# Next gate product ahead of the down products, the sample maps' factor in ScalarE's copy, and two convolution steps on GpSimd

## The chip, the cores and the metric

One NeuronCore of a Trainium2 chip runs the whole program. The metric is device microseconds of one execution. TensorE (PE in the profile), VectorE (DVE), ScalarE (ACT) and GpSimd (POOL) each run their own instruction stream in order, SyncE (SP) issues weight loads, and the streams meet through semaphores.

## The reference, cut to what matters

One layer of a decoder for 1024 prompt tokens and 8 x 4 sample tokens, width 1024. Four mixers (a gated convolution, pooling, sparse top-k attention, differential attention) are followed by an output projection, then this gated MLP of width 2816, then a gated embedding:

```python
xn2 = rmsnorm(h, W['norm_ffn'][i])
g_conv, new_ffn = causal_dwconv(ffn_buf, xn2 @ W['w_gate'][i], W['conv_ffn'][i])   # 3 taps along tokens
h = h + (jax.nn.silu(g_conv) * (xn2 @ W['w_up'][i])) @ W['w_down'][i]
# differential attention: two softmax maps, the second times -lambda
a = probs(q1, k1) - lam * probs(q2, k2);  o = a @ v;  y_d = rmsnorm(o, subln) * (1 - lam_init)
```

## The kernel before, in words

Tokens are split: part a is the first 384 (`NA`), part b the other 672. In the middle of the program two things run interleaved on all engines: the **mixers** of part b, and the **dense** work, which there is the MLP of part a. The MLP has 22 chunks `f` of 128 hidden columns. Of each, TensorE makes a gate product (`"g"`), an up product (`"u"`), and, per 4 chunks (f below `FSPLIT` = 12) or per 2 chunks (from 12 on), 8 down products (`"d"`) that are added to the residual `H`. Chunks below 12 multiply in plain fp32 (8 products of 384 columns, 16 records in the trace); later ones use a high/low split of weights and rows, 24 products, and each weight block must first be split by ScalarE (`wh`, L596) and VectorE (`wl`, L603).

`QUANTA` lists the products in the order in which TensorE makes them, and alternate products use two PSUM banks (`bank(6 + n % 2)`). So product n first waits until product n-2 is read out (`freed`): a gate product by ScalarE's copy (`ag_cp`, L927), an up product by VectorE's multiplication (`a_mul`, L993), a down product by VectorE's addition into `H` (`h_ffn_a`, L977). In between, for each chunk, VectorE convolves the gate row (`dve_gate_conv`: the last two columns are kept in `gtail` L1021, first tap L1022, two more taps L1023 and L1024), ScalarE takes a tanh (L932), VectorE multiplies (L985, then L993 with the up product).

The interleaving is written out by a planner. The mixers' items are numbered n; each has four **places** (p = 0 to 3), and every engine's stream is generated place by place, so an engine does all its work of one place before that of the next. `ISSUED` spreads the dense products over places by their columns; the tables `FREE_AT`, `CONV_AT`, `TANH_AT`, `MUL_AT` and so on give each step of a chunk its place: about one place after what it needs, or earlier when a limit (the place where product n+2 starts) comes first. In one place an engine does `*_free` first, then the mixers' part, then `*_dense`; in a ScalarE place before the change the top-k counting (`act_stage`, L1386) belongs to the mixers' part.

The mixers: in stage one (places 156 to 251) part b runs differential attention with 20 prompt items and 4 sample items (`sdiff`), beside the bitwise top-k search, whose 31 steps are shared by VectorE (L1317) and ScalarE (L1386). In stage two (from place 252) it runs the sparse attention, and the MLP chunks from 12 on. For each item PE makes logits (place 4n), VectorE masks and takes maxima, ScalarE exponentiates (4n+2), VectorE combines the maps (`dve_finish`, 4n+3, for `sdiff` L1866 scales 64 x 1056 values), PE transposes (4n+6, 4n+7), ScalarE copies them (L1726, L1728), PE multiplies by values (4n+9). For tiles of prompt items VectorE's `dve_tile` makes squares, GpSimd a power (L1983), VectorE the product (L1889).

GpSimd's stream (`pool_mixers`) also issues in place order the DMAs that fetch pages of keys and values (L2034, L2042, L2049, L2050) through registers.

## Time and profile before

| what | value |
|---|---|
| three runs | 1745.3, 1760.32, 1759.58 us, median 1759.58 |
| profiled execution | 1758.01 us, of which the trace spans 1756.3 us |
| PE busy | 1630.0 us (93%), mean granted clock 0.969 |
| DVE busy | 1121.2 us (64%) |
| ACT busy | 682.9 us (39%) |
| POOL busy | 214.2 us (12%) |
| chain that ended last | PE 72%, DVE 14%, issue 6%, ACT 6% |

Busy time is the union of an engine's instructions. In the trace stage one lies at about 436 to 752 us from the start of the span and stage two at 752 to 1042 us; what follows is the output projection, the MLP and the embedding of part b. A line number with an engine names an instruction by the source line that issued it; many PE products share L859, and are told apart by their operands.

### The profile page before, as it was taken

To read this page: it belongs to the slowest core of one execution; us is meant where nothing else is said; L and a number is where in the kernel's file an instruction comes from. 1 tells how busy PE (TensorE), PEld (TensorE's weight loads), DVE (VectorE), ACT (ScalarE), POOL (GpSimd) and SP (SyncE) were. 2 spreads that over 40 slices of the span, in tenths; PEclk is the share of its full clock that TensorE was granted. 3 is DMA by queue.
4 is the path that set the end of the run, shared out by engine and by line. 5 is a ranking of instruction groups with operands and counts; after the bars stand their busy time and mean duration, and the time that the engine had idled before them with its cause. 6 is when DMAs were issued, how large, how long until landed. Compare 5 with 4: busy or idle time off the path is not lost.

```text
span 1756.3 us, 26856 instructions
## 1 busy us (share of the span) xinstructions
PE 1630.0 (93%) x9433; PEld 1393.2 (79%) x9433; DVE 1121.2 (64%) x2415; ACT 682.9 (39%) x1289; POOL 214.2 (12%) x360
## 2 busy tenths in 40 slices
PE   6989998998979898899889989899999999999996
PEld 5978897973535445467687889899999999999995
DVE  6466866377788978875556564655555555556845
ACT  5333443354367367433333433432222222223531
POOL 1000000031313222353331010000000000000000
PEclk9999999998989998999989999999999999999998
DMA  5331222241524323323222133122221222222313
GB/s 195 120 108 49 61 79 74 70 156 61 178 76 129 115 93 103 108 63 96 79 91 71 60 114 113 63 73 88 70 69 69 70 71 72 72 72 86 99 61 111
DMA packets 52815, 158.32 MB, mean 90 GB/s; under 512 B 9776, under 2 KB 13872, under 8 KB 52704
## 3 DMA queue, kind: packets, MB, share of 16 engines
q1 hardware_dynamic: 37840, 121.37, 20.6%
q0 software_dynamic: 14864, 35.53, 6.6%
q8 instruction: 62, 1.02, 0.2%
q14 instruction: 49, 0.40, 0.1%
HBM read 147.10 MB, written 9.76 MB: 89 GB/s over the span
## 4 chain that ended last, share of the span: by engine, by line
PE 72%; DVE 14%; issue 6%; ACT 6%; DMA 1%; POOL 0%; SPq 0%; DVEq 0%; POOLq 0%; ACTq 0%
PE ps L859 26%; PE ps L2116 22%; PE ps L2303 9%; DVE junk_b L1317 3%; PE ps L1582 2%; PE ps L1536 2%; ACT act_junk L1386 2%; PE ps L1613 1%; DVE Pb_b L1826 1%; PE ps L1191 1%; DVE wl L603 1%; PE ps L2477 1%; ACT wh L596 1%; DVE SC L1223 1%; PE ps L1593 1%
## 5 line engine op out<-in xcount | busy, mean ns | idle before, releaser
L603 DVE TENSOR_TENSOR wl<-wr,wh 128x1024 fp32r<-128x1024 f32 x176 | 215.3, 1223 | 247.9 <-ACT wh L596 247.3
L596 ACT ACTIVATE wh<-wr 128x1024 fp32r<-128x1024 f32 x176 | 186.1, 1057 | 443.7 <-PE ps L2116 222.3
L2116 PE MATMUL ps<-xh_b,wh 128*128 128x336 f32 x960 | 305.9, 319 | 7.4 <-DVE wl L603 3.3
L2116 PE MATMUL ps<-xl_b,wh 128*128 128x336 f32 x960 | 306.2, 319 | 0.0
L2116 PE MATMUL ps<-xh_b,wl 128*128 128x336 f32 x960 | 304.4, 317 | 0.0
L2116 PEld LDWEIGHTS ps<-xh_b,wh 128*128 128x128 f32 x960 | 182.0, 190 | 9.1 <-DVE wl L603 4.0
L2116 PEld LDWEIGHTS ps<-xh_b,wl 128*128 128x128 f32 x960 | 182.1, 190 | 0.0
L2116 PEld LDWEIGHTS ps<-xl_b,wh 128*128 128x128 f32 x960 | 181.8, 189 | 0.0
L859 PE MATMUL ps<-x_a,wr 128*128 128x384 f32 x384 | 150.8, 525 | 4.2 <-DVE H L977 4.2
L859 PE MATMUL ps<-xh_a,wh 128*128 128x384 f32 x400 | 139.5, 349 | 9.6 <-ACT H L900 3.9
L859 PE MATMUL ps<-xl_a,wh 128*128 128x384 f32 x400 | 137.5, 344 | 0.8 <-DVE H L977 0.8
L859 PE MATMUL ps<-xl_b,wh 128*128 128x336 f32 x352 | 114.8, 326 | 0.0
L859 PE MATMUL ps<-xh_b,wh 128*128 128x336 f32 x352 | 114.5, 325 | 0.0
L859 PE MATMUL ps<-xh_b,wl 128*128 128x336 f32 x352 | 114.1, 324 | 0.0
L859 PEld LDWEIGHTS ps<-x_a,wr 128*128 128x128 f32 x384 | 70.3, 200 | 52.7 <-issue 22.3
L1317 DVE TENSOR_SCALAR_CACHE_REDUCE junk_b<-SC,tk_b 32x1056 uint16<-32x1056 uint16 (+7 forms) x105 | 107.5, 1024 | 6.7 <-DMA SC<-score_spill 3.0
L2303 PE MATMUL ps<-al_b,wh 128*128 128x336 f32 x352 | 111.6, 317 | 0.0
L2303 PE MATMUL ps<-ah_b,wh 128*128 128x336 f32 x352 | 111.3, 316 | 0.2 <-DVE H L2387 0.2
L2303 PE MATMUL ps<-ah_b,wl 128*128 128x336 f32 x352 | 111.4, 316 | 0.0
L1386 ACT ACTIVATE act_junk<-SC,tk_b 128x1024 bf16<-128x1024 uint16 (+2 forms) x93 | 93.4, 1004 | 40.2 <-DVE tk_b L1367 29.0
L2387 DVE TENSOR_TENSOR H<-H,ps 128x336 f32<-128x336 f32 x176 | 85.0, 501 | 33.3 <-PE ps L2303 31.4
L859 PEld LDWEIGHTS ps<-xh_a,wh 128*128 128x128 f32 x400 | 75.9, 190 | 21.9 <-issue 15.0
(420 smaller groups left out, 3153.7 us busy)
## 6 DMA issues: line engine op xcount, KB each, us to landing
wr<-in_weights SPq DMA_DIRECT2D x212, 512.0 KB, 3.4
pages<-in_d_pages POOLq DMA_DIRECT2D x64, 128.0 KB, 2.4
values<-in_d_pages POOLq DMA_DIRECT2D x64, 128.0 KB, 2.5
pages<-in_c_pages POOLq DMA_DIRECT2D x128, 32.0 KB, 2.1
H<-in_xT SPq DMA_DIRECT2D x8, 336.0 KB, 9.1
H<-in_xT POOLq DMA_DIRECT2D x8, 336.0 KB, 5.9
out_y<-Y_out_b SPq DMA_DIRECT2D x8, 336.0 KB, 2.3
H<-in_xT SPq DMA_DIRECT2D x8, 192.0 KB, 4.9
```

Source lines behind the costliest of these rows:

```text
L596: nc.scalar.activation(wh[:, slot], wr[:, slot], ACT.Copy).then_inc(w_hi, 1)
L603: nc.vector.tensor_tensor(wl[:, slot], wr[:, slot], wh[:, slot].bitcast(f32), ALU.subtract).then_inc(w_lo, 1)
L859: last = nc.tensor.matmul(out[:, cols], w, x, start=j == 0, stop=j == count - 1)
L1191: last = nc.tensor.matmul(bank(2 * (u % 2) + h)[:, 0:w], Z[r, QI + p, i * P:(i + 1) * P], Z[r, KI2, a:a + w], start=True, stop=True)
L1223: last = nc.vector.scalar_tensor_tensor(dst, r[:, h], weight, dst, ALU.mult, ALU.add)
L1317: return nc.vector.tensor_scalar(self.junk[0:rows, 0:S], src, scalar, 0.0, op, ALU.add, accum_out=self.col(CNT, j, rows))
L1386: nc.scalar.activation(out[:, 0:S], self.half(j, k >= 15), ACT.Sign, bias=self.col(NBIAS, j), accum_out=self.col(CNT, j)).then_inc(self.ac ...
L1536: last = nc.tensor.matmul(flat(u + m)[:, a:a + w], H[part, q, i * P:(i + 1) * P], Z[part, k, a:a + w], start=True, stop=True)
L1582: last = nc.tensor.matmul(bank(5)[:, HD * h:HD * h + HD], pt[:, b * P:(b + 1) * P], v, start=b == 0, stop=b == i)
L2116: last = nc.tensor.matmul(bank(first_bank + c)[:, 0:CB], w, x, start=k == 0 and t == 0, stop=k == KC - 1 and t == 2)
L2303: last = nc.tensor.matmul(down_bank(v), w, x, start=q == 0 and t == 0, stop=q == 1 and t == 2)
L2387: nc.vector.tensor_tensor(cols, cols, down_bank(v), ALU.add).then_inc(h_ffn, 1)
```

## The change

Four edits. (1) The order of the products: before it was g(f), u(f), downs; now the gate product of the next chunk follows u(f) and stands ahead of the down products, except over the border between chunks 11 and 12 and after chunk 21. The weight blocks follow the same order, and the planner's tables are derived from the new list. (2) For `sdiff` items VectorE no longer scales the 64 x 1056 map: it makes the factor only, at place 4(n+1)+1 and no longer 4n+3, and ScalarE's copy of the 64 x 256 output is given it as scale. The transposes of `sdiff` and `dsa` items wait for the exponentials and no longer for VectorE. (3) From chunk 1 on GpSimd makes the first tap and the copy of the last two columns; VectorE waits for the tap, ScalarE's tanh for the copy. (4) ScalarE's counting goes to the end of each place, behind the dense part; the last product of a differential tile (L1889) goes from place p = 2 to the end of p = 3.

```diff
-for f in range(FC):
-    ...
-    add_chunk(f)
-    if 4 <= f < FSPLIT:
+def add_downs(f):
+    if f == FSPLIT - 1 or 4 <= f < FSPLIT:
         add_down(f // 4 - 1, f % 4)
     elif f >= FSPLIT + 2:
         add_down(down_of(f) - 1, f % 2)
     elif f >= FSPLIT:
         add_down(QUADS - 1, 2 + f - FSPLIT)
+
+for f in range(FC):
+    ...
+    if f in (0, FSPLIT) or not (1 if f < FSPLIT else 1):
+        add_product("g", f)
+    add_product("u", f)
+    if (1 if f < FSPLIT else 1) and f + 1 not in (FSPLIT, FC):
+        add_product("g", f + 1)
+    add_downs(f)
@@ act_dense
                 act.wait_ge(ag_conv, f + 1)
+                if f:
+                    act.wait_ge(ag_tail, f)
                 nc.scalar.activation(ge_a[:, f % 2, 2:2 + NA], gv_a[:, f % 2, 0:NA], ACT.Tanh).then_inc(ag_tanh, 1)
+        def pool_gate_tap(pool, f):
+            e, v, w = ge_a[:, f % 2], gv_a[:, f % 2, 0:NA], half_conv[:, 3 * f:3 * f + 3]
+            pool.wait_ge(ag_conv, f)
+            pool.wait_ge(ag_cp, f + 1)
+            if f >= 2:
+                pool.wait_ge(a_mul, f - 1)
+            nc.gpsimd.tensor_scalar(v, e[:, 0:NA], w[:, 0:1], None, ALU.mult).then_inc(ag_tap, 1)
+            nc.gpsimd.tensor_copy(gtail[:, f], e[:, NA:NA + 2]).then_inc(ag_tail, 1)
@@ dve_gate_conv
-            nc.vector.tensor_copy(gtail[:, f], e[:, NA:NA + 2])
-            link(nc.vector.tensor_scalar(v, e[:, 0:NA], w[:, 0:1], None, ALU.mult))
+            if f:
+                dve.wait_ge(ag_tap, f)
+            else:
+                nc.vector.tensor_copy(gtail[:, f], e[:, NA:NA + 2])
+                link(nc.vector.tensor_scalar(v, e[:, 0:NA], w[:, 0:1], None, ALU.mult))
@@ pe_transposes
-                pe.wait_ge(combined, real(n) + 1)
+                pe.wait_ge(exp_done if kind in ("sdiff", "dsa") else combined, real(n) + 1)
@@ act_sample
-                last = nc.scalar.activation(so_rows[0:64, :], use_at(("so", n))[0:64, 0:256], ACT.Copy)
+                act.wait_ge(combined, real(n) + 1)
+                factor = cf[0:64, 2 * (n % 2):2 * (n % 2) + 1]
+                last = nc.scalar.activation(so_rows[0:64, :], use_at(("so", n))[0:64, 0:256], ACT.Copy, scale=factor)
@@ dve_maxima
-                dve.wait_ge(combined, real(n))
+                dve.wait_ge(combined, real(n) - (ITEMS[n - 1][0] == "sdiff"))
@@ dve_finish
-                    link(nc.vector.tensor_tensor(k, k, small[0:rows, 33:34], ALU.mult))
-                nc.vector.tensor_scalar(logits(n)[0:rows, 0:NK], logits(n)[0:rows, 0:NK], k, None, ALU.mult).then_inc(combined, 1)
+                    nc.vector.tensor_tensor(k, k, small[0:rows, 33:34], ALU.mult).then_inc(combined, 1)
+                else:
+                    nc.vector.tensor_scalar(logits(n)[0:rows, 0:NK], logits(n)[0:rows, 0:NK], k, None, ALU.mult).then_inc(combined, 1)
@@ dve_tile, and the new function that takes its last product
-                dve.wait_ge(head_rstd, diff_tiles(n) + 1)
-                nc.vector.tensor_tensor(heads(yt[:, :]), heads(ot[:, :]), rs4[:, 16:20].unsqueeze(2).to_broadcast([P, 4, HD]),
-                                        ALU.mult).then_inc(yt_ready, 1)
+        def dve_head_norm(dve, n):
+            if ends_tile(n) and ITEMS[n][0] == "diff":
+                heads = lambda x: x.rearrange("p (h d) -> p h d", d=HD)
+                dve.wait_ge(head_rstd, diff_tiles(n) + 1)
+                nc.vector.tensor_tensor(heads(yt[:, :]), heads(ot[:, :]), rs4[:, 16:20].unsqueeze(2).to_broadcast([P, 4, HD]),
+                                        ALU.mult).then_inc(yt_ready, 1)
@@ dve_mixers
             if p == 1:
                 dve_stage(dve, link, n, 1)
+                if kind_of(n - 1) == "sdiff":
+                    dve_finish(dve, link, n - 1)
...
             if p == 3:
                 dve_stage(dve, link, n, 3)
-                dve_finish(dve, link, n)
+                if kind_of(n) != "sdiff":
+                    dve_finish(dve, link, n)
+                dve_head_norm(dve, n - 2)
@@ pool_mixers
             n, p = divmod(place, 4)
+            for f in CONV_AT.get(place, ()):
+                if f:
+                    pool_gate_tap(pool, f)
@@ the ScalarE stream, once per place; the calls of act_stage inside act_mixers are gone
                 act_dense(act, place)
+                act_stage(act, *divmod(place, 4))
```

## Rows read from the trace of the kernel before

**Rows 1.** Busy time by stage, stage one and two; after TensorE's clock, DMA share, GB/s.
```profile
core 0: us, PE busy (x) PEld busy (x) DVE busy (x) ACT busy (x) POOL busy (x), PEclk, DMA share, GB/s
436.00:752.00 316.00, 278.91 (x1222) 150.49 (x1223) 268.27 (x695) 177.50 (x381) 91.80 (x165) 0.94 0.35 112
752.00:1042.00 290.00, 270.79 (x1566) 218.66 (x1565) 169.81 (x338) 104.99 (x212) 68.09 (x107) 0.96 0.25 79
```

**Rows 2.** PE's waits in stage two: waiter, releaser, us in total, times, longest.
```profile
PE ps L859 <- issue: 15.8, 10, 4.6
PE ps L859 <- DVE wl L603: 2.5, 2, 1.5
PE ps L859 <- DVE H L977: 0.8, 1, 0.8
```

**Rows 3.** Timeline of two of these waits: start, duration, engine, instruction, idle before.
```profile
941.28 0.55 DVE L985 SCALAR_TENSOR_TENSOR gv_a<-ge_a,gv_a 128x384 f32<-128x384 f32 x1
941.86 0.56 DVE L993 TENSOR_TENSOR gu_a<-gv_a,ps 128x384 f32<-128x384 f32 x1
942.52 0.42 PE L859 MATMUL ps<-gs_a,wh 128*128 128x384 f32 x1 [1.75 <-issue]
...
860.33 0.66 PE L859 MATMUL ps<-gs_rest_a,wh 128*128 128x384 f32 x1 [4.59 <-issue]
860.79 0.53 PE L859 MATMUL ps<-gs_rest_a,wl 128*128 128x384 f32 x1
...
871.92 0.34 PE L859 MATMUL ps<-xh_a,wh 128*128 128x384 f32 x1
```

**Rows 4.** Clock by stretch, behind two of the gaps.
```profile
857.00:864.00 7.00, 3.67 (x9) 2.60 (x10) 4.34 (x8) 1.47 (x2) 2.50 (x5) 0.60 0.15 36
888.00:899.00 11.00, 9.54 (x54) 8.56 (x53) 5.30 (x10) 1.73 (x5) 1.43 (x3) 0.55 0.03 7
```

**Rows 5.** PE's waits in stage one.
```profile
PE ps L1617 <- ACT PT_b L1728: 6.4, 1, 6.4
PE ps L1617 <- DVE ot L1883: 6.1, 2, 3.5
PE ps L859 <- DVE H L977: 4.2, 3, 2.3
PE ps L1617 <- DVE Pb_b L1866: 3.4, 2, 2.6
PE ps L859 <- issue: 2.8, 2, 1.8
```

**Rows 6.** DVE groups in stage one: count, busy us, mean ns, idle before.
```profile
L1022 DVE TENSOR_SCALAR gv_a<-ge_a,half_conv 128x384 f32<-128x384 f32 x11 | 4.6, 415 | 0.2 <-issue 0.2
L1866 DVE TENSOR_SCALAR Pb_b<-Pb_b,tiny 64x1056 f32<-64x1056 f32 x4 | 3.0, 761 | 0.1
L1021 DVE COPY gtail<-ge_a 128x2 f32<-128x2 f32 x11 | 1.8, 164 | 3.2 <-ACT ge_a L927 3.2
L1889 DVE TENSOR_TENSOR yt<-ot,tiny 128x256 f32<-128x256 f32 x4 | 1.7, 425 | 4.6 <-POOL tiny L1983 4.6
L1353 DVE TENSOR_TENSOR tk_b<-tk_b 128x12 f32<-128x12 f32 x31 | 5.2, 169 | 10.5 <-ACT act_junk L1386 10.5
```

**Rows 7.** ACT and DVE groups in stage two.
```profile
L603 DVE TENSOR_TENSOR wl<-wr,wh 128x1024 fp32r<-128x1024 f32 x30 | 36.6, 1220 | 13.6 <-ACT wh L596 13.4
L596 ACT ACTIVATE wh<-wr 128x1024 fp32r<-128x1024 f32 x31 | 32.6, 1053 | 12.7 <-DMA wr<-in_weights 12.5
L1683 ACT ACTIVATE Pb_b<-Pb_b,tiny 128x1024 f32<-128x1024 f32 x6 | 6.8, 1139 | 0.0
L927 ACT ACTIVATE ge_a<-ps 128x384 f32<-128x384 f32 x11 | 5.4, 489 | 15.2 <-PE ps L859 15.0
L1713 ACT ACTIVATE H<-ps 128x128 f32<-128x128 f32 x10 | 2.2, 275 | 22.5 <-PE ps L1637 22.5
L1713 ACT ACTIVATE H<-ps,subln 128x128 f32<-128x128 f32 x2 | 0.6, 363 | 4.0 <-PE ps L1637 4.0
```

**Rows 8.** POOL timeline: two elementwise instructions at the start, one page fetch.
```profile
14.83 0.94 POOL L2653 MEMSET CM<- 128x1024 f32 x1
15.93 0.81 POOL L2655 TENSOR_SCALAR_AFFINE_SELECT CM<-CM 128x128 f32<-128x128 f32 x1 [0.16 <-POOL CM L2653]
...
516.20 0.54 POOL L2034 DMA_DIRECT2D pages<-in_d_pages  x1 [0.60 <-issue]
```

More of the change, by code:

```diff
@@ L114, with add_product @@
 SKIPPED = []
-def add_chunk(f):
-    for kind in ("g", "u"):
-        ORDER.append(ff_block(kind, f))
-        if f < FSPLIT:
-            SKIPPED.append(len(ORDER) - 1)
-        QUANTA.append((kind, f, 0, KC if f < FSPLIT else 3 * KC, len(ORDER) - 1))
+def add_product(kind, f):
+    ORDER.append(ff_block(kind, f))
+    if f < FSPLIT:
+        SKIPPED.append(len(ORDER) - 1)
+    QUANTA.append((kind, f, 0, KC if f < FSPLIT else 3 * KC, len(ORDER) - 1))
 def add_down(g, part):
@@ L138, in down_of @@
     return f // 4 if f < FSPLIT else QUADS + (f - FSPLIT) // 2
-for f in range(FC):
-    if f == FSPLIT:
-        for part in range(2):
-            add_down(QUADS - 1, part)
-    add_chunk(f)
-    if 4 <= f < FSPLIT:
+def add_downs(f):
+    if f == FSPLIT - 1 or 4 <= f < FSPLIT:
         add_down(f // 4 - 1, f % 4)
@@ L151 @@
         add_down(QUADS - 1, 2 + f - FSPLIT)
+for f in range(FC):
+    if f == FSPLIT:
+        for part in range(2):
+            add_down(QUADS - 1, part)
+    if f in (0, FSPLIT) or not (1 if f < FSPLIT else 1):
[4 more added lines that the diff above has]
+    add_downs(f)
 for part in range(2):
@@ L746, in build @@
         ag_cp, ag_conv, ag_tanh, a_mul = sem("gate_copied_a"), sem("gate_convolved_a"), sem("gate_tanh_a"), sem("gate_times_up_a")
+        ag_tap, ag_tail = sem("gate_first_tap_a"), sem("gate_tail_a")
         h_ffn_a = sem("residual_mlp_a")
@@ L754, in real, with kind_of @@
             return sum(item[0] != "none" for item in ITEMS[:max(n, 0)])
+        def kind_of(n):
+            return ITEMS[max(n, 0)][0]
         def maps_of(n):
@@ L1783, in act_mixers @@
                     act_tile(act, n - 4)
-                act_stage(act, n, 1)
             if p == 2:
@@ L1790, in act_mixers @@
                 act_exp(act, n)
-                act_stage(act, n, 2)
                 if n == QIS_STEP:
@@ L1801, in act_mixers @@
                     act_sample_back(act, n - 2)
-                act_stage(act, n, 3)
             for m in range(KC):
```

## The prediction

> **What bounds the kernel now.** The page's shares say PE with 93%, but the change touches only the two interleaved stages, so I read busy time by stage first. In stage one (316 us) PE is busy 279 us and DVE 268 us [rows 1]: neither is alone the bound, and each stall of one tends to reach the other. In stage two (290 us) PE is busy 271 us against 170 us of DVE and 105 us of ACT: PE is the bound, and only its gaps and its clock can be won. The rest of the program, 1150 us, holds none of the edited steps.
>
> Next, PE's waits. In stage two 15.8 of its 19 idle us are "issue", that is, a wait for which the view names nobody [rows 2]. The timeline names it: DVE's last gate multiplication ends at 942.42 and PE, idle 1.75 us, restarts 0.1 us later with a down product [rows 3]. It is the **bank wait**: in the order g(f), u(f), d0, d1, product d1 is two behind u(f) and needs u(f) read out by L993, while one down product lasts about 1 us (six products 0.17 to 0.2 us apart). DVE has the pair L985, L993 (1.1 us) to do by then, and behind whatever else its place holds; once the gap was 4.59 us.
>
> Then the clock. Stage two has a mean granted clock of 0.96 [rows 1]: 290 x 0.04 x 2 = 23 us at the lower of the two levels, 1.2 instead of 2.4 GHz, hence up to 11.6 us lost. Where it falls is behind gaps: around the 4.59 us gap the stretch reads 0.60, around the next ones 0.55 [rows 4], and products read 0.53 us there and 0.34 us at the full clock [rows 3]. Stage one reads 0.94, up to 19 us lost on PE.
>
> **Part 1, the order.** By the planner's rules applied to the new list, g(f+1) (24 products, three places) now lies between u(f) and d0, so L993 has three places, about 3 x 3.0 us (290 us over some 96 places), before d0 needs it. The convolution and tanh of g(f+1) fall under the down products and u(f+1), long before L985. Of 10 unnamed gaps, 15.8 us, one stays: after u(21) no gate product follows, and its gap (1.75 us, as in rows 3) I leave. Gained: 14.0 us. In stage one the same wait costs 2.8 us [rows 5]; gained 2.8.
>
> The added wait: d1 is now two behind g(f+1), so it needs ScalarE's copy, 0.49 us [rows 7], at the start of the very place in which d1 begins. Behind ACT's copy are queued that place's transposed copies and exponentials, and d2 follows when DVE has added d0. With ACT idle PE loses nothing, since d0 takes 1 us. With an exponential (1.14 us) or a split (1.05 us) ahead of the copy it loses 1 to 2 us; by the planner's places that meets one or two of the 9 chunks, and DVE's addition of d0 now lacks the cover that the old gap gave it: the two other named waits, 3.3 us, are of this kind [rows 2]. From below 0, from above the whole 14.0 us. I take 0.5 us for each of 9 chunks, 4.5 us, nearer to ACT's free case since ACT is busy 105 of 290 us.
>
> The clock should follow the gaps: I take 6 us of the 11.6 (between 0 and 11). Weight loads keep their beat of 24 products per block, and slots are freed in the same rhythm: one block per 290 / 30 = 9.7 us against load, L596 and L603 (1.05 + 1.22 us); cost nothing, hidden by two blocks of products.
>
> Stage two: -14.0 - 6 + 4.5 = **-15.5 us**.
>
> **Part 2, the samples' factor.** DVE loses 4 x 0.76 = 3.0 us [rows 6], on the path twice, as PE waited 3.4 us for L1866 [rows 5]. ScalarE's copy with a scale from memory: 0.36 against 0.28 us for 128 x 128 [rows 7], 4 x 0.1 us, hidden. The `dsa` transposes no longer wait for DVE, but no such wait is in stage two [rows 2]; nothing gained.
>
> **Part 3, the tap on GpSimd.** DVE loses 0.415 us and, as the 2-column copy of 0.164 us overlaps it, about 0.5 us per chunk: 10 chunks in stage one, 5 us; 11 in stage two, where DVE is not the bound, 0. GpSimd's cost isn't in the trace. 1024 columns of memset took 0.94 us, 128 of an affine select 0.81 us [rows 8]: by columns 384 lie between 0.35 and 2.4 us. I take 1.0, since the select's time at 128 columns looks mostly fixed. The tap stands one place after ScalarE's copy, a place lasts 316 / 96 = 3.3 us, and ahead of it in the queue stand one or two fetches of 0.54 + 0.60 us [rows 8]: 3.3 us at most if GpSimd is level with DVE, so hidden. Fetches queued behind the tap now wait for it; their keys are needed at least three places later, hidden too.
>
> The Trainium skill, "GPSIMD Engine Reference", section "Engine selection", speaks against this part: elementwise work belongs on VectorE. Its section "Elementwise — side-by-side cycle accounting" gives 1.8 cycles per element at 1.2 GHz for the best loop, so an estimate by that page is 384 x 1.8 / 1.2 = 576 ns; the sum would be the same, as the tap stays hidden.
>
> **Part 4, ScalarE's counting last, and L1889 later.** DVE waited 4.6 us for GpSimd's power, and 10.5 us for ScalarE's counts [rows 6]. The first is gained, as a whole stage of DVE's work now lies between. The second may grow by tanh going ahead (11 x 0.5 us at the worst) and shrinks nowhere; but DVE's work between is as long. I take 0 (between 0 and +5).
>
> Stage one: DVE is relieved of 3.0 + 5 + 4.6 = 12.7 us. As DVE is one of two near-equal bounds I take half, 6 us, and with 2.8 of part 1: **-9 us** (between 0 and -18; the 19 us of low clock aren't counted, since DVE sets the pace there).
>
> **Sum.** -15.5 - 9 = -24.5 us against the profiled execution's 1758.0 us, which the median tops by 1.6: 1733.5 + 1.6 = **1735 us**. The forecast's own range: all gaps, all clock and 18 us in stage one give -14 - 11 - 18 = -43, 1717; the weak ends up to 1742.
>
> **The rivals.**
> *The copy takes the wait's place* (0.22). d1 stalls for ScalarE or d2 for DVE nearly as long as d1 did for L993: 9 x 1.2 = 11 us come back and the gaps keep the clock low. Left: 14 - 11 + 1 = 4 in stage two and 9 in stage one, 1746 us. For it speaks that every bank wait in the new order has one place of slack or none; against it that ACT is idle for two thirds of the stage.
>
> *The shared input* (0.08). While GpSimd runs, DVE's instructions slow down. The tap and copy of some 1.4 us in each of 10 chunks would take back up to 14 us of the 12.7 that DVE gained in stage one; left there 2 to 3 us: 1742 us or a little more. No row shows the two side by side. The Trainium skill, "GPSIMD Engine Reference", section "Key points", states such contention for DVE instructions with two SBUF inputs; L603, L1023 and L1024 are such.
>
> *GpSimd is late* (0.08, the slower side). The tap waits in a queue that is itself held by fetches and by waits for DVE and PE. From 1.2 us of lateness per tap (24.5 / 21) the gain is gone. If GpSimd comes to each place a full place late, DVE stands 2.3 us (two fetches) beyond its slack in each of 21 chunks: +48 - 24.5 = +24, 1783 us. For it: fetches fill most of GpSimd's time right behind its long waits. Against it: those waits are few, and GpSimd is busy 92 of 316 us.
>
> *Nothing changes* (0.05): stage one is a chain of search steps and stage two finds another unnamed wait, 1757 us.
>
> **How the numbers follow.** The forecast has 0.57. Faster by over 1% (what a measurement of this kernel can tell) means below 1742: 0.57 and a part of the two middle rivals, 0.63. Slower by over 1%, above 1777: 0.07. Within: 0.30. The range leaves out GpSimd late and the best corner: 1716 to 1757.
>
> **What would show it.** Right: stage two's unnamed waits before down products fall from 15.8 to under 4 us and its clock rises from 0.96 to 0.98 or more; L1889 has no wait; DVE waits under 0.2 us for a tap; stage one is 5 to 12 us shorter. Wrong: down products waiting for L927 or L977 by over 8 us; L1023 idle on GpSimd; L603 above 1.22 us; stage one as long as before with more waiting for L1386.

## The result, and the profile after

The changed kernel takes 1707.97 us (median of 4 runs, 1706.3 to 1710.77) against 1756.12 us of the kernel before on the same chip (4 runs): ratio 0.9737, 95% interval 0.9687 to 0.9786, so about 46 us faster. The forecast was 1735 us, with 1716 as the lower end of the range: the measured time lies below the whole range. The sign was right, the size was about half of what came.

The page after. The first line is the engines' busy time, the second TensorE's granted clock in 40 slices (in tenths), the third the chain that ended last; dots stand for lines left out.

```profile
PE 1612.5 (94%) x9433; PEld 1386.2 (81%) x9433; DVE 1108.9 (65%) x2369; ACT 682.2 (40%) x1289; POOL 255.5 (15%) x402
...
PEclk9999999998999998999999999999999999999997
...
PE 72%; DVE 15%; issue 6%; ACT 5%; DMA 1%; POOL 0%; SPq 0%; POOLq 0%; DVEq 0%; ACTq 0%
```

The chain's shares are those of before. Where the time went is seen only by stage. From here on a stage is cut at the same three instructions in every kernel: the first product of `kring` and `qis`, the first 64-column logits product of a sparse-attention item, the first `xh_b` product of 336 columns behind it. By these cuts the kernel before reads (columns as in [rows 1]):

```profile
436.49:760.03 323.54, 286.93 (x1263) 156.06 (x1263) 273.89 (x707) 180.70 (x387) 95.35 (x171) 0.94 0.35 112
760.03:1047.19 287.16, 264.73 (x1535) 214.70 (x1534) 167.91 (x330) 106.74 (x212) 64.55 (x100) 0.96 0.25 80
```

and the changed kernel:

```profile
434.49:735.88 301.39, 276.13 (x1262) 152.05 (x1262) 265.67 (x681) 180.56 (x388) 106.98 (x183) 0.97 0.37 119
735.88:999.53 263.65, 256.98 (x1535) 210.06 (x1534) 163.63 (x310) 105.87 (x211) 94.10 (x131) 0.99 0.29 88
```

Stage one is 22.1 us shorter, stage two 23.5 us, what lies behind them the same (709.1 us before, 709.6 after). Stage one also begins 2.0 us earlier, but nothing ahead of it was changed, and in the runs below it begins anywhere between 429.7 and 436.5 us; so this is not counted as gain. In either stage TensorE's gain has two parts: less idle time (36.6 to 25.3 us, 22.4 to 6.7 us) and less busy time for the same products (286.9 to 276.1 us, 264.7 to 257.0 us), as the granted clock rose from 0.94 to 0.97 and from 0.96 to 0.99.

PE's waits in stage two after, for [rows 2]:

```profile
PE ps L870 <- issue: 3.0, 5, 1.8
PE ps L870 <- DVE H L990: 0.4, 1, 0.4
```

and from the timeline the one gap that was to stay, behind u(21), for [rows 3]:

```profile
983.83 0.41 PE L870 MATMUL ps<-gs_a,wh 128*128 128x384 f32 x1 [1.75 <-issue]
```

L870 is the dense product (before L859), L990 the addition into `H` (before L977). Of 15.8 us unnamed waits 3.0 are left, 1.75 of them that last gap, and no product waits for ScalarE's copy.

Five of PE's waits in stage one after, for [rows 5]:

```profile
PE ps L1643 <- DVE ot L1909: 10.2, 4, 6.0
PE ps L1639 <- ACT so L1731: 4.4, 2, 3.9
PE ps L1639 <- DVE Pb_b L1881: 3.0, 4, 1.2
PE ps L870 <- issue: 2.2, 2, 1.5
PE ps L870 <- DVE H L990: 0.9, 1, 0.9
```

Two groups of VectorE in stage one, for [rows 6]:

```profile
L1049 DVE SCALAR_TENSOR_TENSOR gv_a<-ge_a,half_conv,gv_a 128x384 f32<-128x384 f32 x11 | 6.8, 616 | 0.7 <-POOL gv_a L1032 0.6
L1379 DVE TENSOR_TENSOR tk_b<-tk_b 128x12 f32<-128x12 f32 x31 | 5.5, 177 | 5.9 <-ACT act_junk L1412 5.8
```

The gate row's copy on ScalarE in stage two, for [rows 7]; it still waits for its product and for nothing else:

```profile
L938 ACT ACTIVATE ge_a<-ps 128x384 f32<-128x384 f32 x10 | 4.9, 489 | 16.0 <-PE ps L870 16.0
```

GpSimd's two new instructions over the whole program:

```profile
L1032 POOL TENSOR_SCALAR gv_a<-ge_a,half_conv 128x384 f32<-128x384 f32 x21 | 33.2, 1583 | 141.5 <-issue 127.0 <-ACT ge_a L938 14.2
L1033 POOL COPY gtail<-ge_a 128x2 f32<-128x2 f32 x21 | 6.9, 329 | 0.0
```

L1049 is the second tap (before L1023), L1379 the step that waits for ScalarE's counts (before L1353). VectorE waits 0.6 us for a tap and 5.8 us for counts, where it was 10.5; the wait for GpSimd's power is gone.

### The profile page after: what moved, and what is told of

Read it like the earlier page. It is cut to its first block, busy times and chain, and to the rows that moved or that the text cites. A ratio compares the mean times of both kernels' runs of the same rounds, so it can differ in the third digit from the quotient of the medians.

```text
span 1709.1 us, 26902 instructions
## 1 busy us (share of the span) xinstructions
PE 1612.5 (94%) x9433; PEld 1386.2 (81%) x9433; DVE 1108.9 (65%) x2369; ACT 682.2 (40%) x1289; POOL 255.5 (15%) x402
## 4 chain that ended last, share of the span: by engine, by line
PE 72%; DVE 15%; issue 6%; ACT 5%; DMA 1%; POOL 0%; SPq 0%; POOLq 0%; DVEq 0%; ACTq 0%
PE ps L870 26%; PE ps L2153 23%; PE ps L2340 9%; DVE junk_b L1343 4%; PE ps L1608 2%; PE ps L1562 2%; PE ps L1639 2%; ACT act_junk L1412 1%; PE ps L1217 1%; PE ps L2514 1%; DVE Pb_b L1851 1%; ACT wh L603 1%; DVE wl L610 1%; DVE SC L1249 1%; PE ps L689 1%
## 5 line engine op out<-in xcount | busy, mean ns | idle before, releaser
L610 DVE TENSOR_TENSOR wl<-wr,wh 128x1024 fp32r<-128x1024 f32 x176 | 215.4, 1224 | 243.2 <-ACT wh L603 242.8
L2153 PE MATMUL ps<-xh_b,wl 128*128 128x336 f32 x960 | 304.1, 317 | 0.0
L870 PE MATMUL ps<-xh_a,wh 128*128 128x384 f32 x400 | 140.3, 351 | 7.3 <-ACT Z L911 2.6
L870 PE MATMUL ps<-x_a,wr 128*128 128x384 f32 x384 | 144.4, 507 | 0.9 <-DVE H L990 0.9
L870 PE MATMUL ps<-xl_a,wh 128*128 128x384 f32 x400 | 138.4, 346 | 0.4 <-DVE H L990 0.4
L870 PE MATMUL ps<-xl_b,wh 128*128 128x336 f32 x352 | 114.9, 326 | 0.0
L870 PE MATMUL ps<-xh_b,wh 128*128 128x336 f32 x352 | 114.6, 325 | 0.0
L870 PE MATMUL ps<-xh_b,wl 128*128 128x336 f32 x352 | 114.1, 324 | 0.0
L2424 DVE TENSOR_TENSOR H<-H,ps 128x336 f32<-128x336 f32 x176 | 85.1, 501 | 33.2 <-PE ps L2340 31.4
L870 PEld LDWEIGHTS ps<-x_a,wr 128*128 128x128 f32 x384 | 68.2, 193 | 46.3 <-issue 14.4
L1412 ACT ACTIVATE act_junk<-SC,tk_b 128x1024 bf16<-128x1024 uint16 (+2 forms) x93 | 93.3, 1003 | 20.7 <-DVE tk_b L1393 18.7
L870 PEld LDWEIGHTS ps<-xh_a,wh 128*128 128x128 f32 x400 | 76.6, 192 | 18.8 <-issue 12.3
```

Of the source, the lines that this page charges most:

```text
L610: nc.vector.tensor_tensor(wl[:, slot], wr[:, slot], wh[:, slot].bitcast(f32), ALU.subtract).then_inc(w_lo, 1)
L870: last = nc.tensor.matmul(out[:, cols], w, x, start=j == 0, stop=j == count - 1)
L1412: nc.scalar.activation(out[:, 0:S], self.half(j, k >= 15), ACT.Sign, bias=self.col(NBIAS, j), accum_out=self.col(CNT, j)).then_inc(self.ac ...
L2153: last = nc.tensor.matmul(bank(first_bank + c)[:, 0:CB], w, x, start=k == 0 and t == 0, stop=k == KC - 1 and t == 2)
L2424: nc.vector.tensor_tensor(cols, cols, down_bank(v), ALU.add).then_inc(h_ffn, 1)
```

## The experiments

Eighteen runs follow; the kernel before was timed anew beside each group of them, and ratios are to that. "Stage" is the length in one profiled execution, cut as above. The changed kernel was profiled twice, and its stages repeat within 0.3 us (run e13); every other kernel has one profile, so how well its stages repeat isn't known. The medians' ratios are uncertain by 0.2 to 0.5% (4 to 9 us), so small parts are read from the stages. The code cuts show the lines that tell an edit, not all of it.

| kernel | median us | ratio, 95% | stage one | stage two |
|---|---|---|---|---|
| before | 1750 to 1756 | 1 | 323.5 | 287.2 |
| changed | 1707.97 | 0.9737 (0.9687 to 0.9786) | 301.4 | 263.7 |
| e1 order alone | 1729.15 | 0.9862 (0.982 to 0.9904) | 316.8 | 268.4 |
| e2 all but the order | 1739.11 | 0.9917 (0.9892 to 0.9942) | 311.6 | 284.3 |
| e3 tap undone | 1712.24 | 0.9771 (0.9731 to 0.9811) | 304.1 | 265.6 |
| e4 counts undone | 1712.62 | 0.978 (0.9742 to 0.9818) | 305.4 | 262.2 |
| e5 factor undone | 1715.96 | 0.979 (0.9748 to 0.9832) | 309.6 | 262.2 |
| e6 tile's last product undone | 1716.41 | 0.9795 (0.9752 to 0.9839) | 307.2 | 265.0 |
| e7 tile earlier | 1710.71 | 0.9761 (0.9717 to 0.9805) | 301.6 | 265.8 |
| e8 tap doubled | 1715.07 | 0.9771 (0.9725 to 0.9817) | 306.1 | 266.0 |
| e9 VectorE padded | 1717.95 | 0.9822 (0.9772 to 0.9871) | 311.1 | 263.7 |
| e10 TensorE padded | 1716.78 | 0.9809 (0.976 to 0.9858) | 311.2 | 263.8 |
| e11 one step to ScalarE | 1715.06 | 0.9804 (0.9755 to 0.9854) | 310.1 | 262.2 |
| e12 more to ScalarE | 1722.79 | 0.9853 (0.9802 to 0.9904) | 314.3 | 262.2 |
| e13 changed again | 1709.59 | 0.974 (0.9703 to 0.9777) | 301.6 | 263.6 |
| e14 changed, weight 0.85 | 1729.9 | 0.9866 (0.9827 to 0.9905) | 314.5 | 270.3 |
| e15 changed, weight 0.80 | 1728.46 | 0.9855 (0.9817 to 0.9892) | 317.1 | 268.7 |
| e16 before, weight 0.85 | 1761.11 | 1.0032 (1.0006 to 1.0057) | 332.6 | 285.2 |
| e17 before, weight 0.95 | 1763.75 | 1.0053 (1.0029 to 1.0077) | 319.0 | 302.4 |
| e18 changed, weight 0.95 | 1730.49 | 0.9863 (0.9814 to 0.9912) | 313.1 | 270.2 |

**Order alone, and all but the order.** In e1 edits 2 to 4 are put back as they were. In e2 only the order is:

```diff
-    if (1 if f < FSPLIT else 1) and f + 1 not in (FSPLIT, FC):
+    if (0 if f < FSPLIT else 0) and f + 1 not in (FSPLIT, FC):
         add_product("g", f + 1)
```

> The kernel before with the new order of products alone: no tap on GpSimd, VectorE still scales the sample maps, counts and L1889 where they were. Theory A (the order frees PE in both stages and its clock comes back with the gaps, in stage one too): 28 to 38 of the 48 us are gained, so about 1725 us; stage two some 23 us shorter and stage one 5 to 14. Theory B (stage one's gain is VectorE's relief alone): stage two 23 us shorter, stage one no more than 3, about 1732 us.

> The changed kernel with the old order of products, all else as changed. Theory A: it keeps 10 to 20 us of the gain, all in stage one; unnamed waits before down products in stage two are back at 14 us or more and its clock at 0.96 to 0.97. Theory B: it keeps 22 us, stage one as short as in the changed kernel.

Windows of e1, stage one and two:

```profile
434.41:751.25 316.84, 283.58 (x1262) 155.48 (x1262) 273.06 (x705) 180.73 (x388) 94.54 (x170) 0.95 0.36 114
751.25:1019.67 268.42, 259.19 (x1535) 211.09 (x1534) 168.54 (x332) 105.76 (x211) 65.58 (x102) 0.99 0.28 86
```

and PE's unnamed waits in its stage two:

```profile
PE ps L870 <- issue: 4.7, 6, 1.9
```

The windows of e2:

```profile
436.18:747.80 311.62, 287.01 (x1263) 155.59 (x1263) 266.91 (x683) 180.55 (x387) 109.16 (x185) 0.93 0.37 116
747.80:1032.12 284.32, 263.99 (x1535) 215.70 (x1534) 163.35 (x308) 106.71 (x212) 87.87 (x128) 0.97 0.27 81
```

and its unnamed waits in stage two:

```profile
PE ps L870 <- issue: 13.6, 9, 4.2
```

Stage two belongs to the order: 18.7 of its 23.5 us come with the order alone, 2.8 with all else alone, and only the kernels with the new order lose the unnamed waits. Stage one divides otherwise: all but the order gives 11.9 us there, with TensorE's busy time where it was (287.0 us) and its clock no better (0.93). All of it is idle time of TensorE (36.6 to 24.6 us). VectorE is busy 7.0 us less (273.9 to 266.9), four waits of it for the power are gone, and the samples' transposes no longer wait for it; how the 11.9 us divide among these isn't shown. The order gives 6.7 us, half of them busy time and half idle time. The unnamed waits have no part in that: in stage one of e1 they are 4.6 us, where [rows 5] had 2.8. Together they give 22.1, which is 3.5 more than the two apart.

**The parts of stage one, each undone alone.** e3: VectorE makes the first tap and the copy again. e4: ScalarE counts inside its mixers' part again. e5: VectorE scales the samples' map again. e6: the tile's last product directly behind the tile.

```diff
 # e3, in the GpSimd stream
-            for f in CONV_AT.get(place, ()):
-                if f:
-                    pool_gate_tap(pool, f)
 # e4, once per place in the ScalarE stream; calls in act_mixers are back
-                act_stage(act, *divmod(place, 4))
 # e5
-                factor = cf[0:64, 2 * (n % 2):2 * (n % 2) + 1]
-                last = nc.scalar.activation(so_rows[0:64, :], ..., ACT.Copy, scale=factor)
+                last = nc.scalar.activation(so_rows[0:64, :], ..., ACT.Copy)
 # e6
                     dve_tile(dve, link, n - 2)
+                    dve_head_norm(dve, n - 2)
...
-                dve_head_norm(dve, n - 2)
```

> The changed kernel with the first tap and the last two columns back on VectorE. Theory A: VectorE has 0.5 us more in each of 10 chunks of stage one; 2 to 5 us slower than the changed kernel. Theory B (VectorE is the bound of stage one): 5 us and more, with the clock's share up to 8. Rival C (GpSimd's 1.25 us for the tap, three times VectorE's 0.415, holds the chain up): 0 to 5 us faster than the changed kernel.

> The changed kernel with ScalarE's counting back in the mixers' part of each place, ahead of the dense part. The prediction took 0 for this edit (0 to 5 us of loss). Theory A: within 2 us of the changed kernel. Rival D (ScalarE's counts ahead of tanh and copies delayed VectorE and PE): 5 to 10 us slower, with VectorE's wait for counts at 10 us again and tanh later.

> The changed kernel with VectorE scaling the four 64 x 1056 sample maps again (L1866's step, at place 4n+3) and the samples' transposes waiting for it. Theory A (each us of VectorE in stage one is worth about half a us, as the run without the tap showed: 5 us back on VectorE, 2.7 us longer): 3.0 us of VectorE give 1.5 us, and PE's direct wait of 2 to 3 us comes back on top: 3 to 5 us slower than the changed kernel. Theory B (VectorE's time alone counts): 1 to 2 us slower.

> The changed kernel with the last product of the differential tile back in place p = 2, where VectorE idles some 1.2 us for GpSimd's power, four times in stage one. Theory A: VectorE's idle time counts half as its work does, 2 to 3 us slower. Rival: it counts in full, 4.6 us or more, since the tile's product stands ahead of a search step on which ScalarE and PE hang.

Stage one gets longer by 2.7, 4.0, 8.2 and 5.8 us. In e4 VectorE waits longer for the counts than the 5.8 us after the change:

```profile
DVE tk_b L1379 <- ACT act_junk L1412: 8.7, 7, 4.5
```

In e5, where the samples' map is scaled by VectorE ahead of its transposes again, TensorE has a wait of the kind that stood first before the change ([rows 5], L1617 for L1728) and one for the scaling (dots for lines left out):

```profile
PE ps L1643 <- ACT PT_b L1754: 7.4, 2, 5.9
...
PE ps L1643 <- DVE Pb_b L1889: 2.1, 2, 1.3
```

In exchange TensorE's wait for L1906, the tile's first step there, is 4.2 us where it was 10.2, and its idle time as a whole grew by only 2.0 us (25.3 to 27.3); the other 6.2 us of e5's price are busy time at a lower clock (0.95). The wait for counts in e4 is no proof of its cause either: it is 9.7 us in e5, which leaves the counting last.

These four prices add to 20.7 us. Undone together they cost 15.5 us (e1 against the changed kernel), and with the old order the four gave 11.9 (e2). So they are not shares of the gain: each says only what is lost from this one arrangement. The run times of e3 and e4 cannot be told from the changed kernel's; those of e5 and e6 lie at the edge of it.

**The largest stall taken away.** TensorE's largest wait in stage one after is 10.2 us for L1909, the tile's first step on VectorE. In e7 VectorE does the whole part of the tile one place earlier, ahead of that place's search step.

```diff
             if p == 1:
+                if n >= 2:
+                    dve_tile(dve, link, n - 2)
                 dve_stage(dve, link, n, 1)
...
             if p == 2:
-                if n >= 2:
-                    dve_tile(dve, link, n - 2)
                 dve_stage(dve, link, n, 2)
```

> The changed kernel with the first part of each tile (reading the outputs' PSUM bank, L1909) at the start of place p = 1's search step and not behind it in p = 2. PE's largest wait left in stage one, 10.2 us in 4 pieces, is for exactly that reading. Theory A (stage one is paced by such single stalls and the low clock behind them): 4 to 9 us faster than the changed kernel, with stage one's clock at 0.98. Theory B (stage one is paced by VectorE's sum of work): within 1 us of the changed kernel, the stall only moves.

Stage one of e7:

```profile
432.58:734.21 301.63, 281.03 (x1262) 155.14 (x1262) 265.66 (x681) 180.67 (x388) 106.43 (x183) 0.96 0.38 119
```

and PE's wait for L1909 in it:

```profile
PE ps L1643 <- DVE ot L1909: 2.4, 2, 2.1
```

The wait fell from 10.2 to 2.4 us and the stage kept its length (301.6): PE's idle time shrank from 25.3 to 20.6 us, and its busy time grew from 276.1 to 281.0 at a lower clock. This stall of TensorE, the largest, was not what set the stage's end.

**The tap doubled.** GpSimd makes the same tap twice, VectorE waits for the second.

```diff
-            nc.gpsimd.tensor_scalar(v, e[:, 0:NA], w[:, 0:1], None, ALU.mult).then_inc(ag_tap, 1)
+            nc.gpsimd.tensor_scalar(v, e[:, 0:NA], w[:, 0:1], None, ALU.mult).then_inc(ag_twice, 1)
+            pool.wait_ge(ag_twice, f)
+            nc.gpsimd.tensor_scalar(v, e[:, 0:NA], w[:, 0:1], None, ALU.mult).then_inc(ag_tap, 1)
```

> The changed kernel with GpSimd making every first tap twice, 1.25 us more in 21 chunks. If the tap is hidden with room (VectorE waited 0.6 us in all) and the two engines do not slow each other: within 2 us of the changed kernel and VectorE's waits for the tap under 3 us. If GpSimd's work slows VectorE through a shared input: 21 x 1.25 = 26 us more GpSimd work, 5 us or more slower, and L1049, L1050 and L610 longer than 619 and 1224 ns. If GpSimd is just in time: up to 26 us slower, in VectorE's waits for the tap.

The second tap on GpSimd, over the whole program:

```profile
L1034 POOL TENSOR_SCALAR gv_a<-ge_a,half_conv 128x384 f32<-128x384 f32 x21 | 29.2, 1389 | 2.0
```

VectorE's two taps and weight split there:

```profile
L1051 DVE SCALAR_TENSOR_TENSOR gv_a<-ge_a,half_conv,gv_a 128x384 f32<-128x384 f32 x22 | 13.6, 617 | 8.2 <-POOL gv_a L1034 8.0
L1052 DVE SCALAR_TENSOR_TENSOR gv_a<-ge_a,half_conv,gv_a 128x384 f32<-128x384 f32 x22 | 13.6, 619 | 0.8
L610 DVE TENSOR_TENSOR wl<-wr,wh 128x1024 fp32r<-128x1024 f32 x176 | 215.3, 1224 | 243.5 <-ACT wh L603 243.0
```

For comparison, the third tap in the kernel before, the second has the same 619 ns:

```profile
L1024 DVE SCALAR_TENSOR_TENSOR gv_a<-ge_a,half_conv,gv_a 128x384 f32<-128x384 f32 x22 | 13.6, 619 | 0.8
```

Twice the work on GpSimd leaves VectorE's instructions with two inputs at 617, 619 and 1224 ns; [rows 7] had the split at 1220. These means hide what the timeline shows: the two engines do wait for each other, and nearly all of it falls on GpSimd. In the changed kernel 12 of the 21 taps take 1.24 to 1.26 us and nine 1.49 to 2.84. Eight of the nine begin while VectorE is in an instruction that reads two tensors in SBUF. Two of them, each with the weight split that was running:

```profile
815.02 1.23 DVE L610 TENSOR_TENSOR wl<-wr,wh 128x1024 fp32r<-128x1024 f32 x1 [0.39 <-ACT wh L603]
815.71 1.65 POOL L1032 TENSOR_SCALAR gv_a<-ge_a,half_conv 128x384 f32<-128x384 f32 x1 [2.73 <-issue]
904.23 1.23 DVE L610 TENSOR_TENSOR wl<-wr,wh 128x1024 fp32r<-128x1024 f32 x1 [0.39 <-ACT wh L603]
904.74 1.83 POOL L1032 TENSOR_SCALAR gv_a<-ge_a,half_conv 128x384 f32<-128x384 f32 x1 [13.20 <-issue]
```

The split has 0.54 us left when the first tap begins, and the tap takes 0.40 us over 1.25; with 0.72 us left the second takes 0.58 over. In e15 1.11 us are left for one tap, and it takes 2.22 us. The 12 short taps begin with at most 0.13 us left of such an instruction, but for one behind an instruction of 32 partitions. Over the 21 taps this is some 7 us of GpSimd's time (33.2 less 21 times 1.25). VectorE pays in four short instructions, 0.7 us in all; the clearest is a product of 384 columns, 0.76 us beside a tap and 0.56 elsewhere, before and after in the mean:

```profile
L1003 DVE TENSOR_TENSOR gs_a<-gu_a,gs_rest_a 128x384 fp32r<-128x384 f32 x6 | 3.3, 556 | 6.4 <-ACT gs_rest_a L935 6.3
L1016 DVE TENSOR_TENSOR gs_a<-gu_a,gs_rest_a 128x384 fp32r<-128x384 f32 x6 | 3.5, 591 | 3.2 <-ACT gs_rest_a L948 3.2
```

The cover ends with the second tap: over the whole program the waits for a tap go from 0.6 to 8.0 us (2.0 in stage one, 6.0 in stage two), stage one from 301.4 to 306.1 us and stage two from 263.7 to 266.0.

**Padding VectorE and TensorE.** e9 makes a reciprocal of one column four times in each item of part b, e10 makes the first slice of each prompt item's logits products twice (the first result is overwritten).

```diff
 # e9
-                link(nc.vector.reciprocal(cf[:, c + 1:c + 2], sm[:, c + 1:c + 2]))
+                for again in range(4 if n >= B_FIRST else 1):
+                    link(nc.vector.reciprocal(cf[:, c + 1:c + 2], sm[:, c + 1:c + 2]))
 # e10
-                        last = nc.tensor.matmul(...)
+                        for again in range(2 if n >= B_FIRST and kind == "diff" and a == 0 else 1):
+                            last = nc.tensor.matmul(...)
```

> The changed kernel with one reciprocal of 0.14 us made four times and not once in each of the 20 prompt items of stage one, some 0.2 us each with the waits between: 9 to 12 us more of VectorE in stage one. Theory B (VectorE paces stage one, its time counts in full): stage one 8 to 12 us longer. Theory A (two near-equal bounds, a half counts): 4 to 6 us longer.

> The changed kernel with the first 512 columns of each logits product of stage one made twice: 40 products of about 0.5 us, some 20 us more of PE in stage one. Theory B (VectorE paces stage one and PE has room): 0 to 6 us longer. Theory A (two near-equal bounds): 8 to 12 us longer. If PE is the bound: 20 us.

Stage one of e9:

```profile
430.77:741.89 311.12, 280.96 (x1263) 154.20 (x1263) 275.25 (x738) 180.81 (x388) 108.56 (x182) 0.96 0.37 115
```

Stage one of e10:

```profile
432.63:743.82 311.19, 296.06 (x1342) 161.23 (x1342) 265.59 (x681) 180.27 (x388) 107.75 (x183) 0.97 0.37 115
```

9.6 us more of VectorE make the stage 9.7 us longer, 19.9 us more of TensorE 9.8 us. At this point I read it as "VectorE counts in full, TensorE by half"; runs e14 to e18 below take the exactness from that reading. So does e9 itself: 4.8 of its 9.7 us are busy time of TensorE for the same products (276.1 to 281.0 us, clock 0.97 to 0.96).

**Counting moved to ScalarE.** VectorE and ScalarE share the six counts of each search step by tables; in e11 VectorE's count of 512 columns goes to ScalarE, in e12 that of 768 columns instead.

```diff
 # e11
-ACT_TOP = [4, 3, 1]
-DVE_TOP = [5, 2, 0]
+ACT_TOP = [4, 3, 1, 0]
+DVE_TOP = [5, 2]
 # e12
+ACT_TOP = [4, 3, 2, 1]
+DVE_TOP = [5, 0]
```

> The changed kernel with one of the six counts of each of the 31 search steps (512 columns) moved from VectorE to ScalarE: VectorE loses 31 x (0.75 + 0.08) = 26 us of stage one, ScalarE gets 31 x (0.7 + 0.19) = 28 us, of 181 busy out of 301. Theory B (VectorE paces stage one): 15 to 25 us faster than the changed kernel, until PE with 276 us binds. Theory A: about 10 us faster. Rival: ScalarE becomes late, VectorE's wait for counts grows from 5.8 us to 20 and more, and nothing is gained.

> As the run before, but the count moved is the one of 768 columns: VectorE loses 31 x (1.01 + 0.08) = 34 us, ScalarE gets 31 x (0.9 + 0.19) = 34 us. If VectorE still paces stage one then, 5 us faster than with 512 columns; if ScalarE or PE has taken over, the same or slower.

Stage one of e11:

```profile
429.70:739.81 310.11, 281.99 (x1263) 155.43 (x1263) 244.00 (x619) 205.33 (x450) 106.40 (x183) 0.96 0.37 115
```

and VectorE's wait for the counts in it:

```profile
DVE tk_b L1379 <- ACT act_junk L1412: 24.1, 12, 4.0
```

VectorE has 21.7 us less to do and waits 18.3 us more for ScalarE: the stage is 8.7 us longer. In e12 the wait is 31.7 us and the stage 12.9 us longer. The search goes step after step over both engines, and here the stage gained nothing from work that VectorE then waited for.

**The same products at shifted places.** The planner spreads the dense products over places, those of stage two with a weight of 0.9. The weight was moved to either side, in the changed kernel (e14, e15, e18) and in the kernel before (e16, e17); e13 is the changed kernel as it is, timed together with e14 and e15. Nothing else is changed: no instruction is added or taken away.

```diff
-... [(p, 1.0 if p < 4 * DSA_B else 0.9) for p in range(FFN_AT, NPOS)])
+... [(p, 1.0 if p < 4 * DSA_B else 0.85) for p in range(FFN_AT, NPOS)])
```

> The changed kernel once more, unchanged, as the measure for the two others of this call. All theories: 0.9737 of the kernel before, about 1708 us; stage one 301.4 and stage two 263.7 us within 1 us each.

> Changed kernel with the planner's weight of stage two's places at 0.85 in place of 0.9: somewhat more of the dense layers' products are issued in stage one. My theory (stage one pays half of what is added to TensorE and all of what is added to VectorE, stage two gives TensorE's time back in full): if 5 us of products move, stage two loses 5 us and stage one gains 2.5 us plus the vector work of the moved layers (some 1.5 us), so 1 us faster, 1707 us. Rival 1, TensorE's time counts in full in both stages: no change in TensorE's part and the vector work on top, 1709 to 1710. Rival 2, stage one has idle room for products on TensorE and they cost nothing there: 4 us faster, 1704.

> Changed kernel with the weight at 0.8: twice the move of the run before. My theory: 2 us faster, 1706 us, with stage one some 8 us longer and stage two some 10 us shorter. Rival 1 (TensorE's time counts in full in both stages): 1711. Rival 2 (room on TensorE in stage one): 1700.

All three theories failed: no move of products by a few microseconds explains 20 us. The changed kernel at 0.85, stage one and two:

```profile
436.37:750.91 314.54, 284.88 (x1274) 156.92 (x1274) 265.64 (x680) 181.49 (x387) 107.37 (x185) 0.96 0.36 115
750.91:1021.18 270.27, 256.83 (x1523) 210.63 (x1522) 162.81 (x311) 105.53 (x212) 88.02 (x128) 0.98 0.27 85
```

and PE's longest waits in stage two:

```profile
PE ps L870 <- issue: 4.5, 5, 2.6
PE ps L1608 <- ACT PT_b L1754: 2.1, 1, 2.1
PE ps L870 <- DVE wl L610: 1.6, 1, 1.6
```

Only 12 product records went from stage two to stage one. VectorE's busy time is the same to 0.1 us and yet stage one is 13.1 us longer; stage two has fewer products and is 6.6 us longer. Both have a lower clock and more idle time on TensorE. So part of what the changed kernel gains at 0.9 may be its places, and the kernel before had to be asked the same.

> The kernel before with the planner's weight of stage two's places at 0.85 in place of 0.9. What it tells: how far the kernel before moves when every dense product is shifted by a fraction of a place. Theory A (the changed kernel's gain holds for the order itself): the old order moves by less than 10 us, 1750 to 1765. Theory B (the kernel before sat in a bad spot of its weight, and part of the 48 us is that spot): at 0.85 or 0.95 the old order is 10 to 20 us faster, 1736 to 1745.

> The kernel before with the weight at 0.95. Theory A: 1750 to 1765. Theory B: this one or the run before is at 1736 to 1745.

> The changed kernel with the weight at 0.95, the other side of 0.9. If 0.9 is a favourable spot of the changed kernel, as 0.85 and 0.80 suggest (20 us slower each): 1718 to 1730. If more products in stage two are right by themselves (stage two pays TensorE's time in full, stage one gains half of it): 1708 to 1712.

The kernel before at 0.85, and then at 0.95:

```profile
434.89:767.49 332.60, 294.70 (x1274) 161.56 (x1275) 273.58 (x707) 181.30 (x388) 95.49 (x171) 0.93 0.35 110
767.49:1052.64 285.15, 263.69 (x1523) 215.53 (x1522) 168.69 (x330) 105.84 (x212) 64.89 (x100) 0.96 0.25 79
```

```profile
430.62:749.58 318.96, 286.15 (x1248) 154.59 (x1248) 273.79 (x706) 181.01 (x387) 95.85 (x171) 0.93 0.35 112
749.58:1052.01 302.43, 278.63 (x1549) 223.42 (x1548) 168.19 (x331) 107.10 (x212) 64.67 (x100) 0.94 0.25 77
```

The changed kernel at 0.95:

```profile
433.43:746.56 313.13, 279.08 (x1248) 153.26 (x1249) 265.78 (x678) 180.62 (x387) 107.31 (x183) 0.95 0.35 113
746.56:1016.71 270.15, 259.62 (x1549) 211.68 (x1548) 164.38 (x313) 106.16 (x213) 87.99 (x130) 1.00 0.28 88
```

No weight tried beats the changed kernel at 0.9. The kernel before was not in a bad spot: to either side it is 6 and 9 us slower. The changed kernel is in a good one: all three neighbours are 19 to 22 us slower. At equal weights the edits give 0.9866 / 1.0032 = 0.983 at 0.85 and 0.9863 / 1.0053 = 0.981 at 0.95, that is 29 and 33 us (each plus or minus 8 to 10 by the intervals), against 46 us at 0.9. By stage, one and two: 22.1 and 23.5 us at 0.9, 18.1 and 14.9 us at 0.85, 5.8 and 32.3 us at 0.95; together 45.6, 33.0 and 38.1 us.

The good spot is seen in the earlier runs too, in which no product changed its place. In e3 to e9, e11 and e12, whatever was altered, TensorE is busy 279.6 to 282.8 us in stage one for the same products, where the changed kernel has 276.1 and 276.4 in its two profiles. So 3.5 to 6.7 us in each of those stage lengths is busy time at a lower clock (0.95 or 0.96 against 0.97), and can't be put down to the one edit.

## Why the prediction was right in sign and wrong in size

**Part 1, the order, in stage two: mechanism right, 15.5 us forecast, 23.5 measured.** The bank wait was the cause: with the order undone the unnamed waits are back (13.6 us, e2), with the order alone they are gone (4.7 us, e1). The gap behind u(21) stayed at 1.75 us as forecast. The term of 4.5 us for d1 behind ScalarE's copy and d2 behind the addition was the one mis-sized: no wait for the copy is in the trace, and L990 is waited for 0.4 us. The two waits for the weight split (2.5 us in [rows 2]) went as well; the sum had not counted them, since the prediction read them as waits for the addition. So TensorE's idle time fell by 15.8 us, where 9.5 were in the sum. The clock term, 6 us, measured 7.7 (busy time 264.7 to 257.0 for the same 1535 records). The clock came with the gaps' end in e1 too: order alone, clock 0.99.

**Stage one: this step failed at the weight of 0.9, 9 us forecast, 22.1 measured.** Three statements of it were wrong.
- "As DVE is one of two near-equal bounds I take half, 6 us": edits 2 to 4 alone give 11.9 us, nearly the whole of the 12.7 that were counted as VectorE's relief (its three terms add to 12.6), with TensorE's busy time unchanged (e2). Near-equal busy shares did not halve it. Why not stays open: e2 also lets the transposes start earlier and counts last, and with 21.7 us taken off VectorE in e11 the stage got longer.
- The order was put at 2.8 us, its unnamed waits; e1 gives 6.7 us, and by another way: the unnamed waits are 4.6 us there and not gone. Half of the 6.7 is busy time at a better clock (0.95), the rest idle time in other waits.
- "The 19 us of low clock aren't counted, since DVE sets the pace there": TensorE's busy time fell by 10.8 us in the stage. How much of that reached the stage's length is not settled. With e10, where 19.9 us of products cost 9.8, about half would; but e7 shows busy time and idle time trading against each other at constant length.

**No term for the place at which things fall: this is the rest.** The sum priced waits and instructions, and took for granted that a step's price holds wherever the planner puts it. A list that differs by one product per chunk gives every step behind it another place. The same instructions at a weight of 0.85, 0.80 or 0.95 cost the changed kernel 19 to 22 us, and at 0.85 or 0.95 the kernel before 6 to 9 us. Of the 46 us, 29 and 33 are had at the neighbouring weights by the medians, 33.0 and 38.1 by the stages; so some 8 to 17 us belong to the arrangement at 0.9, and the intervals of 8 to 10 us don't fix it better. The forecast of 24.5 us is nearer to the first part and knew nothing of the second. Which of the steps meet so well at 0.9 was not isolated: in stage one at 0.85 and 0.95 one sees lower clock (0.96, 0.95), more idle time on TensorE (29.7, 34.1 us against 25.3), and VectorE waiting for counts for 8.6 and 12.7 us against 5.8. That these are causes and not symptoms is argued, not shown.

**Part 2, the factor.** Forecast: 3.0 us less of VectorE, inside the half. Undone, stage one is 8.2 us longer, more than the instructions taken away: with it undone the samples' second product is late behind a chain of scaling, transposes and copy (7.4 and 2.1 us of waits in e5). "On the path twice" was right. What it is worth isn't: 6.0 us of another wait went at the same time, and 6.2 of the 8.2 us are TensorE's busy time at a lower clock, of which every altered kernel has 3.5 us or more.

**Part 3, the tap.** The relief of VectorE and the hiding were right; VectorE waits for a tap once, 0.6 us, against the 0.2 us that the forecast allowed. The duration was not: 1.25 us for most of them and 1583 ns in the mean, against the 1.0 that I took, the mean standing above the usual mostly by waits for two-input instructions of VectorE; the bounds of 0.35 and 2.4 us hold for the mean, the longest tap took 2.84 us. Undoing it costs 2.7 us in stage one and 1.9 in stage two, in this arrangement. The Trainium skill, "GPSIMD Engine Reference", section "Elementwise — side-by-side cycle accounting", led to an estimate of 576 ns by its best loop; the trace has more than twice that. Its rule in "Engine selection", that elementwise work belongs on VectorE, is right by price per instruction (415 ns there in [rows 6]), and did not decide here: GpSimd's tap was waited for once, 0.6 us.

**Part 4, counts last and L1889 later.** The wait for the power is gone, as forecast. "Shrinks nowhere" was wrong: the wait for counts fell from 10.5 to 5.8 us. That the counting's new place did it isn't shown: the wait is 8.7 us with the counting put back (e4), but 6.9 in e1, which never moved it, and 11.6 in e2, which counts last in the old order.

**The rivals.** *The copy takes the wait's place*: refuted, no wait for it in stage two. *The shared input*: its price is refuted, its mechanism is there. The forecast had VectorE slowed by up to 14 us; VectorE loses 0.7 us, and GpSimd's taps lose some 7 us, which the tap's slack hides. The Trainium skill, "GPSIMD Engine Reference", section "Key points", warns of this contention for two SBUF inputs, and the trace agrees: 1.65 and 1.83 us for taps that begin under the split, 1.25 us else. *GpSimd is late*: 0.6 us; one more tap per chunk would begin to make it true (8.0 us, e8). *Nothing changes*: refuted.

## What to carry to other kernels

Where all engines' streams are written out place by place, read every gain at the neighbouring settings of the planner too, for the old kernel and the new one, before a size is believed: here 8 to 17 of 46 us were the spot. Where products alternate over two banks, each waits for the reader of the one two before it: look for unnamed waits, put a product whose cover is long between, and count the clock behind the gaps too. Undoing edits one by one in such a kernel can overprice each of them (20.7 us singly, 15.5 together). And an operation may be three times as dear on an idle engine and still be well placed there, as long as nobody waits for it; but look at its single durations, as the two engines can hold each other up.

## What the hardware showed that was not expected

GpSimd's multiplication of 128 x 384 fp32 by a scalar from memory takes 1.25 us when nothing holds it and 2.84 us at the longest, and its copy of two columns 329 ns in the mean; VectorE has 0.415 and 0.164 us for the same [rows 6]. Most of the excess is what a VectorE instruction with two SBUF inputs, already running, had left, less some 0.14 us (0.54 us left: 0.40 over 1.25). The other way round VectorE lost 0.7 us in all: its second and third tap and its weight split kept 616, 619 and 1224 ns in the mean.

TensorE's busy time is not a constant of its products: in the kernel before at 0.95 stage two has 14 records more than at 0.9 and is busy 13.9 us longer, at a granted clock of 0.94 against 0.96. The changed kernel with those same 1549 records is busy 259.6 us, at 1.00. Idle time and busy time have to be read together, with the clock beside them.
